# Two transformer blocks in fp32 on one core: ScalarE's and VectorE's splitting of weights in another order, and activation rows with the tokens ahead of the meta tokens

## The reference

```python
def first_block(x, ...):
    h = x
    h = h + 0.5 * swiglu(rmsnorm(h, ffn1_norm), w_gate, w_up, w_down)
    n = rmsnorm(h, mix_norm);  z = n @ w_in            # q, k, v and the gated MLP
    ...
    gates = sigmoid(n @ w_gate + b_gate)
    merged = gates[..., :D] * y_attn + gates[..., D:] * y_gmlp
    h = h + merged @ w_out
    h = h + 0.5 * swiglu(rmsnorm(h, ffn2_norm), w_gate2, w_up2, w_down2)
    return rmsnorm(h, final_norm)

def second_block(x, meta_tokens, ...):
    h = concatenate([meta, x])                          # 272 rows
    proj = rms_norm(h, mix_pre_g) @ w_in                # hq, hf, hi, hg, cq, ckv, kpe, gates
    y_a = hgrn2_mixer(hq, hf, hi, hg, ...) @ w_hg_o
    y_b = mla_mixer(cq, ckv, kpe, ...) @ w_mla_o        # cq @ w_q_b, ckv @ w_kv_b, softmax
    mixed = (gate_a * y_a + gate_b * y_b) @ w_out
    h = h + rms_norm(mixed, mix_post_g)
    gt, up = split(rms_norm(h, ffn_pre_g) @ w_ffn_in)
    h = h + rms_norm((silu(gt) * up) @ w_ffn_out, ffn_post_g)
    return h[N_META:]                                   # 256 rows
```

## Time and profile before

| | |
|---|---|
| median of 3 runs | 1037.28 us |
| the profiled execution's own time | 1038.43 us |
| its span on the core | 1036.7 us |
| PE busy | 1024.2 us, 99% |
| DVE busy | 694.4 us, 67% |
| ACT busy | 518.6 us, 50% |
| POOL busy | 97.2 us, 9% |
| PE's share of the chain that ended last | 83% (DVE 8%, ACT 5%) |
| granted TensorE clock, mean | 0.999 |

### The profile page before, as it was taken

One profiled execution on the slowest core, in us unless ns is written; L12 is line 12 of the kernel. 1 busy time (PEld: TensorE's weight loads), 2 busy tenths in 40 slices (PEclk: granted clock), 3 DMA queues, 4 the chain that ended last, 5 costly groups with the idle time before them and its releaser, 6 DMA issues.

```text
span 1036.7 us, 20130 instructions
## 1 busy us (share of the span) xinstructions
PE 1024.2 (99%) x8769; PEld 1005.0 (97%) x8769; DVE 694.4 (67%) x675; ACT 518.6 (50%) x585; POOL 97.2 (9%) x97
## 2 busy tenths in 40 slices
PE   9999999999999999999999999999999999999997
PEld 8999999999999999999999899999999999999997
DVE  6665565767767766565678976697757677656562
ACT  6444444635736554443456476554545554444344
POOL 2000000300200200000022740110000120000001
PEclk9999999999999999999999999999999999999999
DMA  9666656475453647656546553434534535665541
GB/s 309 212 206 195 203 183 202 162 234 163 124 202 123 212 154 235 206 168 202 191 143 184 164 163 111 134 123 125 161 122 163 179 107 176 231 203 176 194 156 41
DMA packets 148240, 179.92 MB, mean 174 GB/s; under 512 B 3981, under 2 KB 135298, under 8 KB 148178
## 3 DMA queue, kind: packets, MB, share of 16 engines
q1 hardware_dynamic: 147504, 177.55, 53.1%
q0 software_dynamic: 400, 1.33, 0.5%
q10 hardware_dynamic: 274, 0.13, 0.0%
HBM read 177.95 MB, written 1.05 MB: 173 GB/s over the span
## 4 chain that ended last, share of the span: by engine, by line
PE 83%; DVE 8%; ACT 5%; issue 3%; DMA 0%; DVEq 0%; ACTq 0%
PE ps L1510 26%; PE ps L1511 25%; PE ps L1512 25%; ACT w_hi L1173 3%; DVE w_lo L1340 3%; PE ps L1918 1%; ACT ar L372 1%; DVE x_lo L1346 0%; DVE ss L1417 0%; DVE ar L1374 0%; DVE ar L1370 0%; DMA ar<-in_vectors_dram 0%; ACT L1149 0%; PE ps L1864 0%; PE ps L1868 0%
## 5 line engine op out<-in xcount | busy, mean ns | idle before, releaser
L1340 DVE TENSOR_TENSOR w_lo<-stage,w_hi 128x2048 fp32r<-128x2048 f32 x164 | 379.9, 2320 | 184.3 <-ACT w_hi L1173 184.1
L1510 PE MATMUL ps<-x_hi,w_lo 128*128 128x256 f32 (+1 forms) x1480 | 416.8, 282 | 2.6 <-DVE w_lo L1340 2.1
L1512 PE MATMUL ps<-x_hi,w_hi 128*128 128x256 f32 (+1 forms) x1480 | 412.9, 279 | 0.0
L1511 PE MATMUL ps<-x_lo,w_hi 128*128 128x256 f32 (+1 forms) x1480 | 412.8, 279 | 0.0
L1173 ACT ACTIVATE w_hi<-stage 128x2048 fp32r<-128x2048 f32 x164 | 311.8, 1906 | 145.8 <-PE ps L1512 145.4
L1510 PE MATMUL ps<-a_hi,w_lo 128*128 128x256 f32 (+1 forms) x1112 | 310.0, 279 | 1.5 <-DVE w_lo L1340 0.9
L1511 PE MATMUL ps<-a_lo,w_hi 128*128 128x256 f32 (+1 forms) x1112 | 308.1, 277 | 0.0
L1512 PE MATMUL ps<-a_hi,w_hi 128*128 128x256 f32 (+1 forms) x1112 | 308.1, 277 | 0.0
L1510 PEld LDWEIGHTS ps<-x_hi,w_lo 128*128 128x128 f32 x1480 | 278.6, 188 | 9.2 <-issue 6.1
L1512 PEld LDWEIGHTS ps<-x_hi,w_hi 128*128 128x128 f32 x1480 | 278.9, 188 | 0.0
L1511 PEld LDWEIGHTS ps<-x_lo,w_hi 128*128 128x128 f32 x1480 | 278.2, 188 | 0.1
(11 more groups left out here) (309 smaller groups left out, 811.4 us busy)
## 6 DMA issues: line engine op xcount, KB each, us to landing
stage<-in_w_in_dram SPq DMA_DIRECT2D x36, 1024.0 KB, 5.3
stage<-in_ffn_w_down_dram SPq DMA_DIRECT2D x22, 1024.0 KB, 5.0
stage<-in_w_ffn_in_dram SPq DMA_DIRECT2D x22, 1024.0 KB, 5.1
stage<-in_ffn_w_gate_dram SPq DMA_DIRECT2D x21, 1024.0 KB, 5.3
stage<-in_ffn_w_up_dram SPq DMA_DIRECT2D x21, 1024.0 KB, 5.3
stage<-in_w_ffn_out_dram SPq DMA_DIRECT2D x11, 1024.0 KB, 5.0
stage<-in_w_gate_dram SPq DMA_DIRECT2D x8, 1024.0 KB, 5.6
stage<-in_w_out_dram SPq DMA_DIRECT2D x8, 1024.0 KB, 5.1
```

What stands on the lines that cost most here:

```text
L1340: nc.vector.tensor_tensor(o, i, b.bitcast(F32), ALU.subtract).then_inc(s["lo_ready"], 1)
L1510: nc.tensor.matmul(o, wl, xh, start=start, stop=False, skip_group_check=skip)
L1511: nc.tensor.matmul(o, wh, xl, start=False, stop=False, skip_group_check=skip)
L1512: return nc.tensor.matmul(o, wh, xh, start=False, stop=stop, skip_group_check=skip)
```

## The change

**Rows.** In `x_hi` and `x_lo` the tokens now stand first (columns 0 to 255) and the meta tokens at 256 to 271. The small tile `warm` (64 bytes per partition) has moved ahead of them, so the tokens keep their addresses: in a partition they begin at byte 90688, as before, and rows that take in the meta tokens also begin there instead of at 90624. The latent rows of `kv_part` have a stride of 320 words instead of 272. PSUM results of 272 columns now have their meta columns last; DVE therefore evicts these 16 columns apart from the 256 (`evict_meta`), in ten further small instructions, since the targets keep meta first. The special place of a pair's hidden part, so laid that an unfinished slab is not overwritten, is now used for J0 and not for J0 + 1.

**FFN starts (all three).** ACT and DVE have another order up to the end of pair J0 + 1.

**Kernel start.** ACT splits slab 2 ahead of the table of the square root. DVE copies only the last turned pair, splits slab 2, and then copies the other three.

**Mixer 1.** At i = 21 both halves are multiplied and added before the low part of either.

**Mixer 2.** At its start the mean's matmuls follow on the whole of slab 1; the splits of slab 3 are ahead of the square roots and of the reciprocal. At i = 6 to 8 DVE splits a slab one step later each; the reciprocal `inverse(7)` has gone from i = 7 to i = 28. POOL's 16 instructions on `h` follow on the scan's levels.

**Kernel end.** DVE adds up all eight squared chunks; PE sums over partitions in 2 matmuls instead of 12 (L1630).

The core of the diff:

```diff
+        warm = sb("warm", [P, 16], F32)
         x_hi = sb("x_hi", [P, DC, X_ROW], F32R)[:, :, 0:L2]
         x_lo = sb("x_lo", [P, DC, X_ROW], F32R)[:, :, 0:L2]
-        warm = sb("warm", [P, 16], F32)
...
-            if J == PAIRS * f + 1:
-                return strided((a_hi, a_lo)[part][:] if f == 0 else (x_hi, x_lo)[part], 1040 if f == 0 else 32, [304, 2], [1, SEQ])
+            if J == PAIRS * f:
+                return strided((a_hi, a_lo)[part][:] if f == 0 else (x_hi, x_lo)[part], 1040 if f == 0 else 272, [304 if f == 0 else 368, 2], [1, SEQ])
...
         def kv_part(v):
-            return v[:].rearrange("p c t -> p (c t)")[:, 512:512 + 2 * L2].rearrange("p (c t) -> p c t", c=2)
+            return strided(v[:], 512, [X_ROW, 2], [1, L2])
...
@@ mixer 1, DVE, i == 21 @@
                             nc.vector.tensor_tensor(tC[:, v], tC[:, v], tD[:, v], ALU.add).then_inc(s["merged1b"], 1)
+                        for half in range(2):
                             dve.wait_ge(s["merged1b"], half + 1)
                             merged_lo(1 + half, 4 + 2 * half, 6 + 2 * half)
...
@@ mixer 2, DVE @@
+            def evict_meta(dst, src, r):
+                nc.vector.tensor_tensor(dst[:, :, 0:META], src[:, :, SEQ:L2], bc(r[:, 0:META], dst.shape[1]), ALU.mult)
...
+            split_lo(n + 3)
             inverse(6, R2, std[:, 1, :])
-            split_lo(n + 3)
...
-                if i == 6:
+                if i in (6, 7, 8):
                     split_lo(n + i + 2)
-                if i == 7:
+                if i == 28:
                     inverse(7)
...
-                if i not in (5, 37, 42):
+                if i not in (5, 6, 7, 37, 42):
                     split_lo(n + i + 3)
...
@@ POOL, mixer 2: these lines now behind the scan's levels @@
             pool.wait_ge(s["xlo_done"], 32)
+            pool.wait_ge(s["o_lo"], 2)
             fg = vec[:, VEC["final_norm"]:]
             for c in range(DC):
                 nc.gpsimd.tensor_scalar(h[:, c, :], h[:, c, :], fg[:, c:c + 1], None, ALU.mult).then_inc(s["x2_done"], 1)
...
@@ ACT, start of an FFN @@
-                gate(J0, n)
-                hidden(J0, n + 1)
-                for b in range(2):
-                    gate(J0 + 1 + b, n + 2 + 3 * b)
-                    hidden(J0 + 1 + b, n + 3 + 3 * b)
-                    split_hi(n + 4 + 3 * b + 3)
+                split_hi(n + 3)
+                silu(J0)
+                split_hi(n + 4)
+                hidden_hi(J0, n + 1)
+                split_hi(n + 5)
+                silu(J0 + 1)
+                split_hi(n + 6)
+                hidden_hi(J0 + 1, n + 3)
+                split_hi(n + 7)
+                gate(J0 + 2, n + 5)
+                hidden(J0 + 2, n + 6)
+                split_hi(n + 10)
...
@@ ACT, kernel start @@
+            split_hi(2)
             load_table(ACT.Sqrt)
-            split_hi(2)
...
@@ ACT, start of mixer 2 @@
             load_table(ACT.Sqrt)
+            split_hi(N_MIX2 + 3)
             act.wait_ge(s["mean_done"], 4)
...
-            split_hi(N_MIX2 + 3)
...
@@ DVE, start of an FFN @@
+                gate_out(J0, n, first=True)
+                split_lo(n + 3)
+                up_out(J0, n + 1, first=True)
+                hidden_both(J0)
+                hidden_lo(J0)
+                split_lo(n + 4)
+                gate_out(J0 + 1, n + 2)
+                up_out(J0 + 1, n + 3)
+                split_lo(n + 5)
+                hidden_both(J0 + 1)
+                split_lo(n + 6)
+                hidden_lo(J0 + 1)
+                split_lo(n + 7)
...
@@ DVE, kernel start @@
-            for b in range(4):
+            tokens_in(3)
+            split_lo(2)
+            for b in range(3):
                 tokens_in(b)
-            split_lo(2)
...
@@ PE, first_slabs (late=True only in mixer 2) @@
-                mean()
+                if not late:
+                    mean()
                 part(1, (DC - 2, DC - 1)).then_inc(s["slab_used"], 1)
+                if late:
+                    mean()
...
@@ PE, kernel end @@
-                    token_sums(7, "ysq_done")
+                    pe.wait_ge(s["ss_ready"], 7)
+                    for i in range(NT):
+                        last = nc.tensor.matmul(ps[:, 4, SEQ + 2 * i:SEQ + 2 * i + 2], ss[:, 0, X0 + P * i:X0 + P * i + P], ones[:, 0:2], ...)
```

More of the change, by code:

```diff
@@ L1383, in ffn @@
                 dve.wait_ge(s["rstd_ready"], rstd_count)
-                gate(J0, n, first=True)
-                hidden(J0, n + 1, first=True)
-                for b in range(2):
-                    gate(J0 + 1 + b, n + 2 + 3 * b)
-                    hidden(J0 + 1 + b, n + 3 + 3 * b)
-                    split_lo(n + 4 + 3 * b + 3)
+                gate_out(J0, n, first=True)
[11 more added lines that the diff above has]
+                split_lo(n + 7)
+                gate(J0 + 2, n + 5)
+                hidden(J0 + 2, n + 6)
+                split_lo(n + 10)
                 with dve.Fori(0, (PAIRS - 5) // 2) as it:
```

117 lines of the change are left out of this document (72 added, 45 removed).

## The result

The changed kernel took 1029.61 us (median of 4 runs, 1028.41 to 1030.53), the kernel before 1037.41 on the same chip. The ratio is 0.9923 with a 95% interval of 0.991 to 0.9935: 7.8 us less, where 9.4 were forecast and the range went from 1023.8 to 1032.2. The profiled execution took 1029.73 us, its span is 1028.0, 8.7 us less than before.

A forecast was written before the change was run, and what follows sets the result against it. The prediction took PE's start-to-start matmul times plus PE's waits to bound the kernel. Its terms, 0.5 + 1.0 + 1.0 + 1.3 + 1.2 + 3.0 + 0.65 + 0.8 = 9.45 us, gave 1027.9 us, range 1023.8 to 1032.2.

The forecast's parts named there:

- What bounds the kernel: Whole kernel: PE's matmul distances plus its waits set the time; PE busy 1024.2 of 1036.7 us.
- Start and FFN 1: Kernel start to FFN 1: three waits go, a new one of 1.3 to 1.4 appears at slab 3; net 0.5 us gained.
- Mixer 1: Mixer 1, slabs 22 and 23: both waits go, 1.0 us gained, and perhaps 1.0 more from the pace behind them.
- the pace: Mixer 1 behind slab 23: 228 matmuls go on at the fast pace, 4.6 ns less each, 1.05 us gained.
- FFN 2 and 3: Starts of FFN 2 and FFN 3: the waits at slabs 4 and 6 go; 1.3 and 1.2 us gained.
- Start of mixer 2: Mixer 2: 3.0 us gained with slabs 7 and 8; 1.9 up to slab 7, after a new wait of 0.6 there.
- Slabs 7 and 8: Mixer 2: three waits, 1.3 us in all, go as a split and a reciprocal move; 1.3 less 0.2 gained.
- Rows: Matmuls of 272 columns: rows begin 64 bytes further, 125.0 ns against 126.3 to 126.7; 0.8 us gained.
- Rival A: Matmuls of 272 columns at 120 ns, giving 3.3 us instead of 0.8; 1025.8 us in all; chance 32%.
- End: Kernel end: ten of twelve small matmuls go, 1.1 us less, DVE's additions take back about 0.5; 0.65 gained.
- Rival B: Mixer 1, slab 7, FFN 1's start: waits move instead of going, slow pace, place gives nothing; 1031.7 us; chance 14%.
- Rival C: FFN loops take over the slow pace, 5.2 us per FFN; 1038.3 with two loops, 1043.5 with three; chance 5%.

The follow-up runs named there:

- tokens_later: Changed kernel with two of DVE's three token copies and the five small instructions moved behind at kernel start: 1028.22 us, ratio 0.9906.
- undo_rest: Changed kernel with the old order back at FFN 2 and 3 starts, mixer 1 i = 21, mixer 2 start and the end: 1038.4 us.
- four place runs: Changed kernel with only tile places moved, rows of x 0, 128, 192, 96 bytes past a multiple of 256: 1045.5, 1067.44, 1051.78, 1056.09 us.

## Why the prediction was right, and where it was off

- **What bounds the kernel**: right. The gain is waits and distances of PE; DVE is busier than before (697.3 us) and nothing of that shows.
- **Start and FFN 1**: right in sign and in sum (0.47 for 0.5), in part because two sizes that were off cancel: the new wait at slab 3 came as named but cost 1.1 instead of 1.4, and the rest gave 1.6 instead of 1.9. tokens_later shows the cause of most of the wait.
- **Mixer 1**: the waits went (1.0 by undo_rest), but the step "without an interruption the pace of slab 21, which started fast, goes on" failed. Slab 21 itself was slow this time, since the draw fell ahead of it, at slab 20. The term that was mis-sized is the pace: 1.05 forecast, and 0.4 lost there instead of gained. Between traces it swings by 1.9 us.
- **FFN 2 and 3**: 1.28 each for 1.3 and 1.2; undone they cost 1.3 and 0.9.
- **Start of mixer 2**: 2.0 to slab 7 for 1.9, by other parts: the wait of 0.6 before slab 7 did not come, and the slow pace took 0.34. The two belong together, as the row of DVE shows. Slabs 7 and 8 gave 1.5 for 1.1.
- **Rows**: 123 to 124 ns at 272 columns, not 125; 1.2 us in slabs 11 to 22 alone for 0.8 forecast in all. Rival A (120 ns) was wrong. The nearest row was the right guide, but a mixed one, which the prediction took as a row at 64: only the first latent row began there. The second lay 272 words, 1088 bytes, behind it, so at 128 past a multiple of 256. With the new stride of 320 words both begin at 64, and the same 20 distances of slab 7 take 2.47 us (123.4 ns), before 2.50. The rule of the Trainium skill ("TensorE: Matmul & The Clock Gate", section "Back-to-back issue gap"), in which an address has no part, would have given nothing here. The changed kernel and the four place runs show that for this stream the address has a part, with 5.33 to 5.64 us for the same 48 matmuls. Where they differ, the measurement decides.
- **End**: 0.41 for 0.65. The mis-sized term is the count: the prediction took each record for a matmul and let two of twelve remain, 1.1 us less, where four of twelve remained, 0.9 less. What DVE's additions take back, 0.5, was right.
- **Rival B** came neither in its waits nor in its place; only its slow pace in mixer 1 came. **Rival C** is real but showed only behind a wait ahead of the loop, which the change removes, and not behind each such wait. Its 5% rested on three loops that had been fast whatever ran ahead, but there the special slab had stood between, so it was luck in part that it didn't come.

In the sum the pace fell short by 1.4 in mixer 1 and took 0.4 more between slabs 23 and 42 of mixer 2, and the end gave 0.2 less; the rows, slabs 7 and 8, the first slab's arrival and the start of mixer 2 came out better by 1.2. Of the rest, what lies between the profiled executions (8.7 us apart) and the medians (7.8) is mostly the profiled execution of the kernel before, which lay 1.15 above the median in the prediction. That the time missed by only 1.7 (1029.61 for 1027.9) with the pace 1.8 off is thus owed in part to errors that cancel.

## What to carry to other kernels

When one engine is 99% busy, list its waits with what stands ahead of the late instruction in the releaser's queue, and move that: read stretch by stretch in undo_rest, the waits removed here paid nearly what was expected of them (5.7 us of 6), and what is put ahead of a critical instruction costs up to its own length (the copies and small instructions, 2.4 us in DVE's queue, cost PE 1.1). Compare start-to-start distances of the same shape across stages before believing that a busy engine is at its limit. Treat the address at which a tile begins in a partition as a setting to be measured: one small tile's size moved this kernel by 38 us (1029.6 to 1067.4). And when counting matmuls in a trace, compare with the program: some stand there twice.
